# Two position biases: built on the chip and expanded through DRAM, or loaded as rows

## The chip, the cores and the metric

One core of one Trainium2 chip runs the whole program. The metric is the device time in microseconds (us) of one execution. The engines named below are PE (TensorE), DVE (VectorE), ACT (ScalarE), POOL (GpSimd) and SP (SyncE, which here only issues transfers).

## The reference

Two stacked models of width 1024 over 16 learned tokens and 256 input tokens. What matters here is the very first mixer, a gated linear attention (GLA), and the two attentions that add a bias by relative position to their logits:

```
# gated linear attention, chunks of 64 (the first layer)
proj = h @ w_in;  q, k, v, r = split(proj)
log_a = log_sigmoid((h @ w_a1) @ w_a2 + b_a) / 16
...
S = exp(tot) * S + (k * exp(tot - cum)).T @ v;  o = q @ S
# first attention (8 heads, top-64 keys): bias through 32 buckets
bias = rel_bias[rel_bucket(top_idx - qpos)]
# second attention (16 heads, band of chunks of 64)
idx = clip(qi + PAD - kj, MIN_REL, MAX_REL) - MIN_REL
bias = rel_bias_2[:, idx]
```

Both biases depend on the distance between query and key alone, so one line per head (8 lines and 16 lines) holds all of their values, and the bias of each query is a piece of that line, shifted by one element from query to query.

## The kernel before

**The weight stream.** All weights are cut into 386 units of 128 x 1024 float32 (512 KB). A unit goes through three stages: SP loads it into one of four slots of `w_raw` (line 370), ACT rounds it to `w_hi` (line 480), DVE computes the rest `w_lo` (line 1257), and PE does 24 matmuls with it (lines 856 to 858, eight tiles by three products). SP may load unit u+4 into a slot when `w_lo` of unit u is written. ACT and DVE prepare the unit that PE will use three units later (`ahead`). Every engine runs a list written out by hand, in that order: an engine that waits holds up everything behind it, and DVE reads PE's results (`scaled`, line 1273) in the same list in which it prepares weights.

**The first stages.** PE runs units `k` (4), `a1` (1), `v` (8), with four small matmuls `z` in the middle of `v` (line 912), and `q` (4). After the third unit of `q`, `to_tokens(0)` transposes the first chunk's keys and values (line 932). Then comes a loop over five chunks: state matmuls (line 949), `to_tokens` of the next chunk, one unit of `r` and the output matmuls (line 960). The state matmuls of a chunk wait until DVE has copied the transposes (line 1378) and read the last unit of `q` (`q_T`).

**The biases.** After `z`, PE expands `rel_bias` into `line1` (8 x 400, line 915), and DVE copies `line1` and builds `line2` (16 x 384) from `rel2`. POOL then stores each line 128 times into a DRAM scratch (lines 413 and 416), waits for both stores, and goes on with its additions of squares. Later POOL loads `bias1` and `bias2` (lines 427 and 456) from the scratch with an access pattern that starts one element earlier for each query (`skewed`). After `bias2` has landed POOL overwrites one part of it with a mask (line 460). `bm1` (line 438, first attention) and `lg2` (line 1802, second attention) use the biases.

The loads by SP go to the DMA queue q1 (hardware), those by POOL to q0 (software); both use the core's 16 DMA engines.

Of the kernel before, what the change touches and what calls it, by code (L numbers as in the profile page):

```python
# [14 lines left out]
F32 = mybir.dt.float32  # L15
# [6 lines left out]
P = 128  # L22
# [3 lines left out]
SEQ = 256  # L26
T = META + SEQ
# [7 lines left out]
ATT_HEADS = 8  # L35
# [3 lines left out]
HEADS2, HD2 = 16, 64  # L39
NREL2 = 192  # L40
# [1 line left out]

CHUNKS = [(0, META)] + [(META + CHUNK * c, META + CHUNK * (c + 1)) for c in range(SEQ // CHUNK)]
LINE1 = 400
LINE2 = 384
NEG_INADMISSIBLE = -1.0e38
NEG_TAKEN = -3.0e38
MASKED = -1.0e30
# [41 lines left out]

C_ID, C_GSEL, C_HSEL, C_PAIR, C_GBRD = 0, 128, 160, 288, 290
C_HBRD = C_GBRD + 512
C_BUCKET = C_HBRD + 1024
NCONST = C_BUCKET + LINE1


def shape_constants():
    c = np.zeros((P, NCONST), np.float32)
    c[:, C_ID:C_ID + P] = np.eye(P)
    for m in range(KD):  # L100
        c[:, C_GSEL + 4 * m + m // 2] = 1.0
        for half in range(2):
            c[64 * half:64 * half + 64, C_HSEL + 16 * m + 2 * m + half] = 1.0
            c[2 * m + half, C_HBRD + P * m + 64 * half:C_HBRD + P * m + 64 * half + 64] = 1.0
    for half in range(2):
        c[64 * half:64 * half + 64, C_PAIR + half] = 1.0
    for g in range(4):
        c[g, C_GBRD + P * g:C_GBRD + P * (g + 1)] = 1.0
    nb, max_exact, max_dist = 16, 8, 128
    for j in range(LINE1):  # L110
        rel = j - (T - 1)
        n = abs(rel)
        large = max_exact + int(np.float32(np.log(np.float32(max(n, 1)) / np.float32(max_exact)))
                                / np.float32(np.log(max_dist / max_exact)) * (nb - max_exact))
        b = (nb if rel > 0 else 0) + (n if n < max_exact else min(large, nb - 1))
        c[b, C_BUCKET + j] = 1.0
    return c


def build(nc, hT, weights, cols, w_a2, rel_bias, rel2_reversed, constants, outT):  # L120
    ctx = ExitStack()
    with ctx:
        def sb(name, shape, dt=F32):
            return ctx.enter_context(nc.sbuf_tensor(name, shape, dt))
# [8 lines left out]
        h = sb("h", [P, KD, T])  # L133
# [10 lines left out]
        con = sb("con", [P, NCONST])  # L144
# [3 lines left out]
        spl = sb("spl", [P, KD])  # L148
        coef = sb("coef", [P, KD])
        a2 = sb("a2", [RANK, GLA_HEADS * GLA_DK])  # L150
        relb = sb("relb", [32, ATT_HEADS])
        rel2 = sb("rel2", [HEADS2, NREL2])
        line1 = sb("line1", [ATT_HEADS, LINE1])
        line2 = sb("line2", [HEADS2, LINE2])
        ident = con[:, C_ID:C_ID + P]

        def region():
# [59 lines left out]
        bias1 = get("bias1", [P, ATT_HEADS, T])  # L217
# [52 lines left out]
        bias2 = get("bias2", [P, HEADS2, SEQ])  # L270
# [16 lines left out]
        pt = bank("pt")  # L287
# [6 lines left out]

        line1_dram = nc.dram_tensor("line1_dram", (ATT_HEADS, P, LINE1), F32).ap()
        line2_dram = nc.dram_tensor("line2_dram", (HEADS2, P, LINE2), F32).ap()

        def skewed(dram, heads, width, keys):  # L300
            return bass.AP(dram.tensor, P - 1, [[width - 1, P], [P * width, heads], [1, keys]])

        raw_loaded = [sem(f"raw_loaded{s}") for s in range(RING)]
        hi_ready = sem("hi_ready")
        lo_ready = sem("lo_ready")
# [3 lines left out]
        in_loaded = sem("in_loaded")  # L309
# [11 lines left out]
        def s_(name):  # L321
            if name not in sems:
                sems[name] = sem(name)
            return sems[name]
# [29 lines left out]
        @block.sync  # L354
        def _(sp):
            sp.dma_start(par[:, :], cols).then_inc(s_("par_loaded"), 16)
            sp.dma_start(w_raw[:, 0, :], weights[0, :, :]).then_inc(raw_loaded[0], 16)
            for quarter in range(4):
                n = slice(2 * quarter, 2 * quarter + 2)
                sp.dma_start(h[:, n, :], hT[:, n, :]).then_inc(h_loaded[quarter], 16)  # L360
            for u in range(1, RING):
                sp.dma_start(w_raw[:, u, :], weights[u, :, :]).then_inc(raw_loaded[u], 16)
            sp.dma_start(con[:, :], constants).then_inc(in_loaded, 16)
            sp.dma_start(a2[:, :], w_a2).then_inc(in_loaded, 16)
            sp.dma_start(relb[:, :], rel_bias).then_inc(in_loaded, 16)
            sp.dma_start(rel2[:, :], rel2_reversed).then_inc(in_loaded, 16)
            with sp.Fori(1, UNITS // RING) as i:
                for s in range(RING):
                    sp.wait_ge(lo_ready, i * RING + (s + 1 - RING))
                    sp.dma_start(w_raw[:, s, :], weights[bass.ds(i * RING + s, 1), :, :]  # L370
                                 .rearrange("a p n -> p (a n)")).then_inc(raw_loaded[s], 16)
            for u in range(UNITS // RING * RING, UNITS):
                sp.wait_ge(lo_ready, u + 1 - RING)
                sp.dma_start(w_raw[:, u % RING, :], weights[u, :, :]).then_inc(raw_loaded[u % RING], 16)
            for quarter in range(4):
                n = slice(2 * quarter, 2 * quarter + 2)
                sp.wait_ge(acc_free, tile_read("mlp1_out", 2 * quarter + 1))
                sp.dma_start(outT[:, n, :], h[:, n, META:T]).then_inc(s_("out_stored"), 16)
            sp.wait_ge(s_("out_stored"), 64)
# [3 lines left out]
        def _(pool):  # L383
            allt, xt = slice(0, T), slice(META, T)

            def add_squares(norm, tok):
# [22 lines left out]
                                           ALU.add).then_inc(s_("sqg_added"), 1)  # L409

            add_squares("mix0", allt)
            pool.wait_ge(s_("line1_ready"), 1)
            pool.dma_start(line1_dram, line1[:, :].rearrange("h (a w) -> h a w", a=1).to_broadcast([ATT_HEADS, P, LINE1]))\
                .then_inc(s_("line_stored"), 16)
            pool.wait_ge(s_("line2_ready"), 3)
            pool.dma_start(line2_dram, line2[:, :].rearrange("h (a w) -> h a w", a=1).to_broadcast([HEADS2, P, LINE2]))\
                .then_inc(s_("line_stored"), 16)
            pool.wait_ge(s_("line_stored"), 32)
            for c, (lo, hi) in enumerate(CHUNKS):
                pool.wait_ge(s_("osq_ready"), c + 1)  # L420
                pairs = o_sq[:, :, lo:hi].rearrange("p (g two) t -> p g two t", two=2)
# [2 lines left out]
            add_squares("ffn0", allt)  # L424
            add_squares("mix1", allt)
            pool.wait_ge(units_used, FIRST["dsa_c"])
            pool.dma_start(bias1[:, :, :], skewed(line1_dram, ATT_HEADS, LINE1, T))\
                .then_inc(s_("bias1_loaded"), 16)
            for t in range(2 * ATT_HEADS):
                hd, qt = t // 2, t % 2  # L430
# [22 lines left out]
            for norm in ("mlp0", "att2"):  # L453
                add_squares(norm, xt)
            pool.wait_ge(units_used, FIRST["kv2"])
            pool.dma_start(bias2[:, :, :], skewed(line2_dram, HEADS2, LINE2, SEQ))\
                .then_inc(s_("bias2_loaded"), 16)
            pool.wait_ge(s_("bias2_loaded"), 16)

            pool.memset(bias2[0:64, :, 192:256], MASKED).then_inc(s_("bias2_ready"), 1)  # L460

            for k in range(HEADS2):
                n = SEQ if k % 2 else P
# [382 lines left out]
        def _(pe):  # L846
# [58 lines left out]
            unit(FIRST["a1"], FIRST["a1"] % RING, pa[0][:, 0:T], x_hi, x_lo, allt, True, True)  # L905
            four("v", 0, MT["v"], 0, 0, x_hi, x_lo, allt)
            pe.wait_ge(s_("a1_ready"), 1)
            pe.wait_ge(in_loaded, 64)
            for n in range(4):
                if n >= 2:  # L910
                    pe.wait_ge(s_("z_ready"), n - 1)
                nc.tensor.matmul(pa[n % 2][:, 0:T], a2[:, n * P:(n + 1) * P], a1_T[:, :], start=True, stop=True)\
                    .then_inc(s_("z_psum"), 1)

            nc.tensor.matmul(pt[0:ATT_HEADS, 0:LINE1], relb[:, :], con[0:32, C_BUCKET:C_BUCKET + LINE1],
                             start=True, stop=True).then_inc(s_("line1_psum"), 1)
            four("v", 4, MT["v"] + 4, 0, 0, x_hi, x_lo, allt)

            def project_r(k):
# [23 lines left out]
            for c, (lo, hi) in enumerate(CHUNKS):  # L943
# [4 lines left out]
                for g in range(GLA_HEADS):  # L948
# [3 lines left out]
                                     start=True, stop=True).then_inc(s_("S_psum"), 1)  # L952
# [299 lines left out]
        def _(dve):  # L1252
# [81 lines left out]
            for k in range(8):  # L1334
# [1 line left out]
                scaled(v_T[:, k, :], acc[k % 4][:, 0:T], allt)  # L1336
                ahead("v", k)
                if k == 3:
                    dve.wait_ge(in_loaded, 64)
                    for n in range(4):  # L1340
                        dve.wait_ge(s_("z_psum"), n + 1)
                        V.tensor_scalar(z[:, n, :], pa[n % 2][:, 0:T], col("b_a", n), None, ALU.add)\
                            .then_inc(s_("z_ready"), 1)
                    dve.wait_ge(s_("line1_psum"), 1)
                    V.tensor_copy(line1[:, :], pt[0:ATT_HEADS, 0:LINE1]).then_inc(s_("line1_ready"), 1)

                    V.tensor_copy(line2[:, P - 1:P - 1 + NREL2], rel2[:, :]).then_inc(s_("line2_ready"), 1)
                    V.tensor_copy(line2[:, 0:P - 1], rel2[:, 0:1].to_broadcast([HEADS2, P - 1]))\
                        .then_inc(s_("line2_ready"), 1)
                    V.memset(line2[:, P - 1 + NREL2:LINE2], 0.0).then_inc(s_("line2_ready"), 1)  # L1350
                elif k == 5:
                    dve.wait_ge(s_("ln_ready"), 1)

# [428 lines left out]
                copy_values(g)  # L1782
            dve.wait_ge(s_("q2std_ready"), 1)
            own_wait(dve, V.reciprocal(q2rs[:, :], q2std[:, :]))
            dve.wait_ge(s_("bias2_ready"), 1)

            def trail_heads(m):
                dve.wait_ge(s_("o2_hi_ready"), m + 1)
# [132 lines left out]
def prepare(inputs):  # L1921
    inp = {k: np.asarray(v) for k, v in inputs.items()}
    tokens = np.concatenate([inp["meta"], inp["x"][0]], axis=0)
    arrays = {
        "hT": np.ascontiguousarray(tokens.T.reshape(KD, P, T).transpose(1, 0, 2)),
        "weights": weight_stream(inp),
        "cols": parameter_columns(inp),
        "w_a2": np.ascontiguousarray(inp["gla_w_a2"][0]),
        "rel_bias": np.ascontiguousarray(inp["rel_bias"]),
        "rel2_reversed": np.ascontiguousarray(inp["b_rel_bias_2"][0][:, ::-1]),  # L1930
        "constants": shape_constants(),
    }
    return arrays
# [19 lines left out]
```

## Time and profile before

| | |
|---|---|
| median of 3 runs | 1330.34 us (1328.74 to 1331.99) |
| span of the profiled execution | 1327.7 us |
| median less that span | 2.6 us |
| PE busy | 1267.2 us, 95% |
| DVE busy | 842.3 us, 63% |
| ACT busy | 679.1 us, 51% |
| POOL busy | 106.9 us, 8% |
| moved by DMA | 213.11 MB, mean 161 GB/s |

The profile is one execution; its device time isn't listed apart from its span, so the three runs stand for it, and the 2.6 us are what lies around the span and between executions. PE's share alone says that the kernel is bound by PE; where PE stands still or runs at the lower clock is seen only by stretches.

### The profile page before, as it was taken

How to read it: one execution, taken by the hardware profiler on the slowest of the kernel's cores; microseconds unless marked ns; L12 is line 12 of the kernel's file. 1: busy time of each engine (PE TensorE's matmuls, PEld its weight loads, DVE VectorE, ACT ScalarE, POOL GpSimd, SP SyncE). 2: the span in 40 equal slices, each digit the busy share in tenths (PEclk: the TensorE clock that was granted, in tenths of full speed). 3: DMA queues.
4: the chain of work that ended last, by engine and by line, in shares of the span. 5: the costliest groups of instructions: out<-in, count | busy, mean ns of one | idle time of the engine just before them, and what ended most of it. 6: DMA issues, size and time to landing. Idle time of an engine off the chain costs nothing.

```text
span 1327.7 us, 27055 instructions
## 1 busy us (share of the span) xinstructions
PE 1267.2 (95%) x9838; PEld 1218.5 (92%) x9838; DVE 842.3 (63%) x1310; ACT 679.1 (51%) x1096; POOL 106.9 (8%) x119
## 2 busy tenths in 40 slices
PE   8949999999999899999999869999999998999999
PEld 8939899999999679999999769999999876999998
DVE  6626776666557847666667897665556565766543
ACT  5413565554444535666555756554445346665432
POOL 2000010000100111000021121000000012100000
PEclk9969899999999859999999989999999988999999
DMA  7784355555665304556664446556567421555653
GB/s 252 128 160 114 103 169 174 171 172 184 190 208 159 96 0 144 176 187 189 191 201 149 142 128 189 188 180 188 179 184 241 142 78 33 176 188 185 196 179 105
DMA packets 59485, 213.11 MB, mean 161 GB/s; under 512 B 6776, under 2 KB 7944, under 8 KB 59296
## 3 DMA queue, kind: packets, MB, share of 16 engines
q1 hardware_dynamic: 57216, 204.26, 48.8%
q0 software_dynamic: 2208, 8.00, 4.0%
q8 instruction: 42, 0.69, 0.2%
q14 instruction: 19, 0.16, 0.0%
HBM read 206.40 MB, written 5.83 MB: 160 GB/s over the span
## 4 chain that ended last, share of the span: by engine, by line
PE 84%; DVE 8%; issue 2%; DMA 2%; ACT 2%; POOL 1%; SPq 0%; DVEq 0%; POOLq 0%; ACTq 0%
PE acc L856 25%; PE acc L858 25%; PE acc L857 25%; DMA w_raw<-weights 2%; DVE w_lo L1257 2%; PE acc L1084 2%; PE pa L1058 1%; PE acc L949 1%; PE pa L960 1%; POOL sqsum L403 1%; DVE t_s L1680 1%; DVE x_lo L1279 0%; DVE score L1545 0%; PE stat L1074 0%; PE pa L1182 0%
## 5 line engine op out<-in xcount | busy, mean ns | idle before, releaser
L1257 DVE TENSOR_TENSOR w_lo<-w_raw,w_hi 128x1024 fp32r<-128x1024 f32 x383 | 468.6, 1225 | 104.5 <-ACT w_hi L480 104.2
L856 PE MATMUL acc<-x_hi,w_hi 128*128 128x256 f32 (+1 forms) x1792 | 515.1, 287 | 15.3 <-DVE w_lo L1257 12.1
L480 ACT CAST w_hi<-w_raw 128x1024 fp32r<-128x1024 f32 x383 | 398.8, 1045 | 232.8 <-PE acc L858 188.0
L858 PE MATMUL acc<-x_hi,w_lo 128*128 128x256 f32 (+1 forms) x1792 | 511.0, 285 | 0.0
L857 PE MATMUL acc<-x_lo,w_hi 128*128 128x256 f32 (+1 forms) x1792 | 510.7, 285 | 0.0
L856 PEld LDWEIGHTS acc<-x_hi,w_hi 128*128 128x128 f32 x1792 | 341.1, 190 | 22.4 <-issue 15.5
L858 PEld LDWEIGHTS acc<-x_hi,w_lo 128*128 128x128 f32 x1792 | 341.3, 190 | 0.0
L857 PEld LDWEIGHTS acc<-x_lo,w_hi 128*128 128x128 f32 x1792 | 339.8, 190 | 0.3
L857 PE MATMUL acc<-m_lo,w_hi 128*128 128x256 f32 x512 | 144.9, 283 | 0.0
L858 PE MATMUL acc<-m_hi,w_lo 128*128 128x256 f32 x512 | 144.6, 282 | 0.0
L856 PE MATMUL acc<-m_hi,w_hi 128*128 128x256 f32 x512 | 143.5, 280 | 0.0
L857 PE MATMUL acc<-mid_lo,w_hi 128*128 128x272 f32 (+1 forms) x352 | 100.2, 285 | 0.0
L856 PE MATMUL acc<-mid_hi,w_hi 128*128 128x272 f32 (+1 forms) x352 | 100.1, 284 | 0.0
L858 PE MATMUL acc<-mid_hi,w_lo 128*128 128x272 f32 (+1 forms) x352 | 100.0, 284 | 0.0
L856 PEld LDWEIGHTS acc<-m_hi,w_hi 128*128 128x128 f32 x512 | 97.4, 190 | 0.0
L858 PEld LDWEIGHTS acc<-m_hi,w_lo 128*128 128x128 f32 x512 | 96.1, 188 | 0.0
L857 PEld LDWEIGHTS acc<-m_lo,w_hi 128*128 128x128 f32 x512 | 95.7, 187 | 0.0
L1297 DVE TENSOR_TENSOR h<-h,acc 128x256 f32 (+1 forms) x56 | 23.8, 426 | 97.3 <-PE acc L858 97.0
L497 ACT ACTIVATE sq<-h (+1 forms) x64 | 26.4, 422 | 95.8 <-DVE h L1297 95.8
L858 PEld LDWEIGHTS acc<-mid_hi,w_lo 128*128 128x128 f32 x352 | 66.4, 189 | 0.0
L857 PEld LDWEIGHTS acc<-mid_lo,w_hi 128*128 128x128 f32 x352 | 66.2, 188 | 0.0
L856 PEld LDWEIGHTS acc<-mid_hi,w_hi 128*128 128x128 f32 x352 | 66.0, 188 | 0.0
(303 smaller groups left out, 1641.3 us busy)
## 6 DMA issues: line engine op xcount, KB each, us to landing
w_raw<-weights SPq DMA_DIRECT2D x383, 512.0 KB, 3.5
line_dram<-line POOLq DMA_DIRECT2D x1, 3072.0 KB, 69.4
bias<-line_dram POOLq DMA_DIRECT2D x1, 2048.0 KB, 13.7
line_dram<-line POOLq DMA_DIRECT2D x1, 1600.0 KB, 36.5
con<-constants SPq DMA_DIRECT2D x1, 1113.0 KB, 9.6
h<-hT SPq DMA_DIRECT2D x4, 272.0 KB, 4.6
bias<-line_dram POOLq DMA_DIRECT2D x1, 1088.0 KB, 9.1
outT<-h SPq DMA_DIRECT2D x4, 256.0 KB, 4.8
```

Of the source, the lines that this page charges most:

```text
L403: pool.tensor_tensor(flat(sqsum[:, tok]), sq[:, bass.ds(n, 1), tok], flat(sqsum[:, tok]), ALU.add)\
L480: nc.scalar.copy(w_hi[:, slot, :], w_raw[:, slot, :]).then_inc(hi_ready, 1)
L497: nc.scalar.activation(sq[:, nn, tok], h[:, nn, tok], ACT.Square).then_inc(sq_ready, 1)
L856: nc.tensor.matmul(out, wh, xh[:, k, tok], start=first and n == 0, stop=False)
L857: nc.tensor.matmul(out, wh, xl[:, k, tok], start=False, stop=False)
L858: ins = nc.tensor.matmul(out, wl, xh[:, k, tok], start=False, stop=last and n == ntiles - 1)
L949: nc.tensor.matmul(acc[2 + g // 2][:, (g % 2) * GLA_DV:(g % 2 + 1) * GLA_DV], k_tok[0:n, c % 2, g * P:(g + 1) * P], v_tok[0:n, c % 2, g * ...
L960: ins = nc.tensor.matmul(pa[1][:, m * n:(m + 1) * n], S[:, c % 2, m // 2, (m % 2) * P:(m % 2 + 1) * P], q_T[:, m // 2, lo:hi], start=True, ...
L1058: nc.tensor.matmul(pa[qt][:, 0:n], q1[:, hd, qt * P:(qt + 1) * P], kh[:, hd, 0:n], start=True, stop=True).then_inc(s_("qk1"), 1)
L1084: ins = nc.tensor.matmul(acc[hd % 4][:, qt * P:(qt + 1) * P], vh[0:m, b, hd * P:(hd + 1) * P], pt1[0:m, qt, b0:b0 + P], start=(b == 0), st ...
L1257: V.tensor_tensor(w_lo[:, slot, :], w_raw[:, slot, :], w_hi[:, slot, :].bitcast(F32), ALU.subtract)\
L1297: V.tensor_tensor(h[:, nn, tok], h[:, nn, tok], acc[j][:, 0:n_tok].rearrange("p (a t) -> p a t", a=1), ALU.add)\
```

## The change

The host lays both biases out per query and head (`bias1_rows` 128 x 8 x 272, `bias2_rows` 128 x 16 x 256, the mask included) and passes them as inputs. POOL loads them at the same two places of its list as before. The PE matmul for `line1`, DVE's four instructions for the lines, the two stores, POOL's wait for them, the two small loads `relb` and `rel2` and the mask's memset are gone. The constants lose the 400 columns that `line1` needed (1113 KB before, 913 KB after, by their shapes of 128 x 2226 and 128 x 1826). DVE waits for `bias2_loaded` where it waited for `bias2_ready`.

```diff
+def skewed_biases(rel_bias, rel2):
+    at = (P - 1) - np.arange(P)[:, None] + np.arange(T)[None, :]
+    bias1 = rel_bias[bucket_line()[at]].transpose(0, 2, 1)
+    at = np.clip(np.arange(SEQ)[None, :] - np.arange(P)[:, None], 0, NREL2 - 1)
+    bias2 = rel2[:, ::-1][:, at].transpose(1, 0, 2).copy()
+    bias2[0:64, :, 192:256] = MASKED
+    return bias1, bias2
...
-            sp.dma_start(relb[:, :], rel_bias).then_inc(in_loaded, 16)
-            sp.dma_start(rel2[:, :], rel2_reversed).then_inc(in_loaded, 16)
...
-            pool.wait_ge(s_("line1_ready"), 1)
-            pool.dma_start(line1_dram, line1[:, :].rearrange("h (a w) -> h a w", a=1).to_broadcast([ATT_HEADS, P, LINE1]))\
-                .then_inc(s_("line_stored"), 16)
-            pool.wait_ge(s_("line2_ready"), 3)
-            pool.dma_start(line2_dram, line2[:, :].rearrange("h (a w) -> h a w", a=1).to_broadcast([HEADS2, P, LINE2]))\
-                .then_inc(s_("line_stored"), 16)
-            pool.wait_ge(s_("line_stored"), 32)
...
             pool.wait_ge(units_used, FIRST["dsa_c"])
-            pool.dma_start(bias1[:, :, :], skewed(line1_dram, ATT_HEADS, LINE1, T))\
+            pool.dma_start(bias1[:, :, :], bias1_rows)\
                 .then_inc(s_("bias1_loaded"), 16)
...
             pool.wait_ge(units_used, FIRST["kv2"])
-            pool.dma_start(bias2[:, :, :], skewed(line2_dram, HEADS2, LINE2, SEQ))\
+            pool.dma_start(bias2[:, :, :], bias2_rows)\
                 .then_inc(s_("bias2_loaded"), 16)
-            pool.wait_ge(s_("bias2_loaded"), 16)
-
-            pool.memset(bias2[0:64, :, 192:256], MASKED).then_inc(s_("bias2_ready"), 1)
...
-            nc.tensor.matmul(pt[0:ATT_HEADS, 0:LINE1], relb[:, :], con[0:32, C_BUCKET:C_BUCKET + LINE1],
-                             start=True, stop=True).then_inc(s_("line1_psum"), 1)
...
-                    dve.wait_ge(s_("line1_psum"), 1)
-                    V.tensor_copy(line1[:, :], pt[0:ATT_HEADS, 0:LINE1]).then_inc(s_("line1_ready"), 1)
-
-                    V.tensor_copy(line2[:, P - 1:P - 1 + NREL2], rel2[:, :]).then_inc(s_("line2_ready"), 1)
...
-            dve.wait_ge(s_("bias2_ready"), 1)
+            dve.wait_ge(s_("bias2_loaded"), 16)
```

POOL's list at the place of the stores, before (`z` here is the tile `o_sq2`, the sums of squares of the chunk loop; `line` and `line_dram` are the lines and the scratch):

```order
L400 COMPARE_AND_BRANCH
L413 DMA line_dram<-line 1024x1x400
L416 DMA line_dram<-line 2048x1x384
L422 TENSOR_TENSOR z<-o_sq 128x4x16
L422 TENSOR_TENSOR z<-o_sq 128x4x64 x4
```

and after:

```order
L400 COMPARE_AND_BRANCH
L415 TENSOR_TENSOR z<-o_sq 128x4x16
L415 TENSOR_TENSOR z<-o_sq 128x4x64 x4
L395 TENSOR_TENSOR sqsum<-sq 128x272
L400 UNCONDITIONAL_BRANCH
```

Both stores are gone, and nothing takes their place. DVE's list behind the four `z` instructions, before:

```order
L1345 COPY line<-pt 8x400
L1347 COPY line<-rel 16x192
L1348 COPY line<-rel 16x127
L1350 MEMSET line 16x65
L1273 TENSOR_TENSOR v_T<-acc,rstd 128x272
L1257 TENSOR_TENSOR w_lo<-w_raw,w_hi 128x1024
```

and after:

```order
L1261 TENSOR_TENSOR v_T<-acc,rstd 128x272
L1245 TENSOR_TENSOR w_lo<-w_raw,w_hi 128x1024
L1261 TENSOR_TENSOR v_T<-acc,rstd 128x272
L1245 TENSOR_TENSOR w_lo<-w_raw,w_hi 128x1024
L1335 SCALAR_TENSOR_TENSOR z<-z,zabs 128x1088
```

The four instructions for the lines are gone, and the rest keeps its order.

## Rows read from the trace of the kernel before

**Rows 1.** The chain that ended last, in order of time: start us, us, what.
```profile
44.05 0.77 PE pt L915 x2
...
57.49 31.66 DMA w_raw<-weights
...
106.05 1.92 PE acc L949 x8
...
114.16 1.92 PE acc L949 x8
```

**Rows 2.** DMA issues of the page: KB each, us from issue to landing.
```profile
w_raw<-weights SPq DMA_DIRECT2D x383, 512.0 KB, 3.5
line_dram<-line POOLq DMA_DIRECT2D x1, 3072.0 KB, 69.4
bias<-line_dram POOLq DMA_DIRECT2D x1, 2048.0 KB, 13.7
line_dram<-line POOLq DMA_DIRECT2D x1, 1600.0 KB, 36.5
...
bias<-line_dram POOLq DMA_DIRECT2D x1, 1088.0 KB, 9.1
```

**Rows 3.** DMA queues, 46 to 67 us: packets, MB, share of 16 engines.
```profile
q0 software_dynamic: 743, 1.84, 87.2%
q1 hardware_dynamic: 3, 0.01, 0.1%
```

**Rows 4.** Loads of weights issued between 52 and 64 us.
```profile
DMA to landing us min/median/max: 23.1/29.9/34.4
```

**Rows 5.** Waits, 40 to 125 us: us in total, times, longest.
```profile
POOL z L422 <- DMA line_dram<-line: 68.4, 1, 68.4
...
PE acc L949 <- DVE q_T L1273: 10.5, 1, 10.5
...
PE acc L856 <- DVE w_lo L1257: 9.1, 1, 9.1
```

**Rows 6.** Timeline, 66 to 100 us: start us, us, engine, what, [idle before].
```profile
68.39 0.60 PE L932 MATMUL stat<-con,v_T 128*16 128x128 f32 x4
...
78.09 0.57 PE L856 MATMUL acc<-x_hi,w_hi 128*128 128x272 f32 x1 [9.11 <-DVE w_lo L1257]
...
82.91 0.29 PE L858 MATMUL acc<-x_hi,w_lo 128*128 128x272 f32 x1
...
90.24 1.23 DVE L1257 TENSOR_TENSOR w_lo<-w_raw,w_hi 128x1024 fp32r<-128x1024 f32 x1 [5.03 <-ACT w_hi L480]
...
93.66 3.77 PE L949 MATMUL acc<-v_tok,k_tok 16*128 16x256 f32 x8 [10.46 <-DVE q_T L1273]
```

**Rows 7.** Windows: busy of PE, PEld, DVE, ACT, POOL; granted clock, DMA share, GB/s.
```profile
30.00:40.00 10.00, 10.00 (x81) 10.00 (x80) 5.03 (x7) 3.16 (x3) 0.00 (x0) 1.00 0.71 227
...
78.00:83.30 5.30, 5.10 (x24) 4.91 (x24) 0.30 (x1) 0.74 (x1) 0.00 (x0) 0.60 0.99 217
...
93.60:106.00 12.40, 12.34 (x61) 10.67 (x61) 5.94 (x12) 3.48 (x4) 0.00 (x0) 0.63 0.63 120
106.00:114.20 8.20, 8.20 (x62) 7.63 (x62) 5.41 (x12) 2.15 (x6) 0.00 (x0) 1.00 0.61 117
```

**Rows 8.** Loads of weights issued between 990 and 1015 us, beside `bias2`'s load.
```profile
DMA to landing us min/median/max: 3.5/4.5/8.3
```

**Rows 9.** Waits, 990 to 1120 us.
```profile
ACT w_hi L480 <- DMA w_raw<-weights: 0.5, 1, 0.5
```

**Rows 10.** Instructions on `bias1` and `bias2`: duration ns min/median/max, first and last start.
```profile
L438 POOL TENSOR_TENSOR bm<-bias,mask x16: 487/756/1317, 439.5 to 484.3; 128x144 f32<-128x144 f32 x8, 128x272 f32<-128x272 f32 x8
L1802 DVE SCALAR_TENSOR_TENSOR lg<-pa,q2rs,bias x16: 340/342/351, 1080.9 to 1106.0; 128x128 f32<-128x128 f32 x16
...
L427 POOL DMA_DIRECT2D bias<-line_dram x1: 923/923/923, 381.4 to 381.4; - x1
L456 POOL DMA_DIRECT2D bias<-line_dram x1: 1202/1202/1202, 995.5 to 995.5; - x1
```

More of the change, by code:

```diff
@@ L44 @@
 LINE1 = 400
-LINE2 = 384
 NEG_INADMISSIBLE = -1.0e38
@@ L92 @@
 C_HBRD = C_GBRD + 512
-C_BUCKET = C_HBRD + 1024
-NCONST = C_BUCKET + LINE1
+NCONST = C_HBRD + 1024
 def shape_constants():
@@ L108, in shape_constants, with bucket_line @@
         c[g, C_GBRD + P * g:C_GBRD + P * (g + 1)] = 1.0
+    return c
+def bucket_line():
+    buckets = np.zeros(LINE1, np.int64)
     nb, max_exact, max_dist = 16, 8, 128
@@ L115, in shape_constants, with build @@
         b = (nb if rel > 0 else 0) + (n if n < max_exact else min(large, nb - 1))
-        c[b, C_BUCKET + j] = 1.0
-    return c
-def build(nc, hT, weights, cols, w_a2, rel_bias, rel2_reversed, constants, outT):
+        buckets[j] = b
+    return buckets
+def skewed_biases(rel_bias, rel2):
[5 more added lines that the diff above has]
+    return bias1, bias2
+def build(nc, hT, weights, cols, w_a2, bias1_rows, bias2_rows, constants, outT):
     ctx = ExitStack()
@@ L150, in build @@
         a2 = sb("a2", [RANK, GLA_HEADS * GLA_DK])
[L151 to L154, printed above, removed]
         ident = con[:, C_ID:C_ID + P]
@@ L293, in build @@
         trans1 = [pt, stat]
[L297 to L301, printed above, removed]
         raw_loaded = [sem(f"raw_loaded{s}") for s in range(RING)]
@@ L907, in _ @@
             pe.wait_ge(s_("a1_ready"), 1)
-            pe.wait_ge(in_loaded, 64)
+            pe.wait_ge(in_loaded, 32)
             for n in range(4):
@@ L1338, in _ @@
                 if k == 3:
-                    dve.wait_ge(in_loaded, 64)
+                    dve.wait_ge(in_loaded, 32)
                     for n in range(4):
@@ L1343, in _ @@
                             .then_inc(s_("z_ready"), 1)
-                    dve.wait_ge(s_("line1_psum"), 1)
-                    V.tensor_copy(line1[:, :], pt[0:ATT_HEADS, 0:LINE1]).then_inc(s_("line1_ready"), 1)
-                    V.tensor_copy(line2[:, P - 1:P - 1 + NREL2], rel2[:, :]).then_inc(s_("line2_ready"), 1)
-                    V.tensor_copy(line2[:, 0:P - 1], rel2[:, 0:1].to_broadcast([HEADS2, P - 1]))\
-                        .then_inc(s_("line2_ready"), 1)
-                    V.memset(line2[:, P - 1 + NREL2:LINE2], 0.0).then_inc(s_("line2_ready"), 1)
                 elif k == 5:
@@ L1923, in prepare @@
     tokens = np.concatenate([inp["meta"], inp["x"][0]], axis=0)
+    bias1, bias2 = skewed_biases(inp["rel_bias"], inp["b_rel_bias_2"][0])
     arrays = {
@@ L1928, in prepare @@
         "w_a2": np.ascontiguousarray(inp["gla_w_a2"][0]),
-        "rel_bias": np.ascontiguousarray(inp["rel_bias"]),
-        "rel2_reversed": np.ascontiguousarray(inp["b_rel_bias_2"][0][:, ::-1]),
+        "bias1_rows": np.ascontiguousarray(bias1),
+        "bias2_rows": np.ascontiguousarray(bias2),
         "constants": shape_constants(),
```

## The prediction

> **What bounds the kernel now.** I read the page first, then the chain of waits that ended last, then the stretch of that chain that isn't matmuls. PE is busy for 95% of the span, and nearly all of the chain is PE's stream of weight units, so instructions off PE are worth nothing by themselves. The exception stands out in the chain in order of time: one piece of 31.66 us at 57.49 us that is a DMA, a load of weights [rows 1]. An ordinary load of weights lands in 3.5 us [rows 2]. The reader is to see that this piece begins about 10 us after POOL has issued the two stores of the bias lines, and ends while the longer one is still under way (69.4 us to landing) [rows 2].
>
> The DMA view of 46 to 67 us tells why. POOL's queue q0 moved 743 packets and took 87.2% of the 16 engines; SP's queue q1, with the weights, moved 3 packets [rows 3]. The four loads issued between 52 and 64 us landed after 23.1 to 34.4 us [rows 4]. So the stores did not slow the weights down, they kept them out.
>
> The list of waits says who paid. The longest wait, POOL's 68.4 us for the stores, is a decoy: what POOL does next is needed by PE only at the end of the chunk loop. What costs are PE's waits of 9.1 us (for `w_lo`) and 10.5 us (for `q_T`, which stands on DVE behind `w_lo` instructions that wait for late weights) [rows 5]. The timeline gives the places: PE ends `to_tokens(0)` at 68.39 + 0.60 = 68.99, starts the last unit of `q` at 78.09, ends it at 82.91 + 0.29 = 83.20, and starts the state matmuls of chunk 0 at 93.66 [rows 6]. Those of chunk 1 start at 106.05 [rows 1]. Beside the waits there is the clock: 0.60 of full speed in 78.0 to 83.3 us and 0.63 in 93.6 to 106.0, right behind PE's two long pauses, and 1.00 from 106 us on [rows 7]. 0.60 is a mix of the levels 1.2 and 2.4 GHz.
>
> **The change, part by part.** Between 68.99 and 106.05 lie 37.06 us. With the weights on time the same work costs:
>
> - The wait of 9.10 us before the last unit of `q`: none. With loads that land in 3.5 us its weights are there by about 56 us, and `w_lo` follows on DVE's list right after the first `q_T`, before PE is through with the third unit. Saved 9.1.
> - The unit itself: 83.20 - 78.09 = 5.11 us, partly at the lower clock. At full clock 81 matmuls took 10.00 us [rows 7], so 24 take 3.0. Saved 2.1.
> - The pause of 10.46 us before the state matmuls. DVE has three copies of transposes and the last `q_T` to do there, on its list behind one `w_lo`. From that `w_lo` (90.24) to PE's start (93.66) it took 3.4 us [rows 6]: the pause becomes at least 0 and at most 3.4. The `w_lo` and most of the copies can run while PE is in the unit (3.0 us), so only `q_T` is left behind it, and I take 0.5. Saved 10.0.
> - Chunk 0: 106.05 - 93.66 = 12.39 us, against 114.16 - 106.05 = 8.11 us for chunk 1 [rows 1], with the same number of state matmuls, transposes, unit and output matmuls at the full clock. Saved 4.3.
>
> That is 25.5 us. To it comes the `line1` matmul, 0.77 us on the chain itself [rows 1]: the `v` unit behind it starts that much earlier, and everything up to `to_tokens(0)` with it, because DVE and ACT are ahead of PE there. Saved 0.8. Together 26.3.
>
> The rest is costed at nothing. DVE's four instructions for the lines lie under PE's next unit. The 200 KB less of constants, and the two small loads, lie under a start that waits for the sums of squares. The mask's memset and the moved wait for `bias2` lie far ahead of their readers: `bias2` has landed by 995.5 + 13.7 = 1009.2 and is read at 1080.9; `bias1` has landed by 381.4 + 9.1 = 390.5 and is read at 439.5 [rows 2, 10]. The loads could take 49 us and 71 us longer before a reader waits; the cover gone, each further us would cost one. What they can do is hold up weights. The load of `bias2` did so a little: weights beside it took up to 8.3 us [rows 8], and ACT waited 0.5 us for one of them [rows 9], PE not at all. So ACT has 8.3 - 0.5 = 7.8 us of cover for a landing. The bytes are the same after the change, the rows longer (8.7 and 16 KB in one piece, where pieces of about 1 KB were read). No row shows such a load on POOL's queue; between a gain of nothing (PE doesn't wait there now) and the rival's price below, I take 0, since both loads before stand next to it in everything but the length of rows.
>
> **The sum.** Span 1327.7 - 26.3 = 1301.4. The median of the runs is 2.6 us above that span, so 1304.0 for the changed kernel.
>
> One rule is to be weighed here. The row shows 3 packets of weights against 743 of the stores [rows 3]. The Trainium skill, page "DMA: Bandwidth & Descriptors", section "Queues, rings and completion order", says that each DMA engine goes round the queues for which it has work, packet by packet. By that rule the weights would have had every second turn even then, the lateness would have another cause, and the sum would shrink towards the 0.8 us of the matmul. This trace disagrees with it for stores, by the 3 packets.
>
> **The rivals.**
>
> 1. *The new loads keep the weights out as the stores did* (weights of `dsa_c` and `kv2`). For: [rows 3] shows that POOL's queue can do it. Against: its loads of the same bytes did not, with at most 8.3 us for a unit. If weights stood still for the whole 9.1 and 13.7 us, they would be late by 9.1 + 3.5 - 7.8 = 4.8 and 13.7 + 3.5 - 7.8 = 9.4 us at ACT, 14.2 together; two units already prepared for PE take up to 6.0 us of each, which leaves 0 and 3.4. Time 1307 to 1318, say 1313. Chance 5%.
> 2. *The clock doesn't come back.* The last unit of `q` and chunk 0 follow on short matmuls of 16 rows and a short pause, and could run at the lower clock still. Then 2.1 and 4.3 us are not saved: 1310.4. For: both places were low. Against: chunk 1 and later run the same mix at 1.00 [rows 7], and the long pauses ahead of both are gone. Chance 8%.
> 3. *The stores aren't the cause.* The loads would be late because SP's queue stalls by itself, and the change doesn't do what it says. Only 0.8 us would go: 1329.5. Against: loads land in 3.5 us elsewhere. Chance 1%.
> 4. *Slower.* The direct loads could move at the pace of the stores, with the weights shut out. That pace was 1.84 MB in 21 us, 88 GB/s [rows 3]: 1.11 MB and 2.10 MB would take 12.7 and 23.9 us, and ACT would be late by 8.4 and 19.6, 28.0 together and 1.7 more than is saved: 1332.0. Under 85 GB/s the kernel would be slower by over 0.2%. Against: the loads landed at 122 and 153 GB/s, with weights moving beside them [rows 2, 8]. Chance 1%.
>
> **How the numbers follow.** The forecast itself has 85%. Its range: the pause before chunk 0 (-0.5 to +2.9 us), the bias loads (0 to 3.4), where PE's short spells of the lower clock fall once all is shifted (some 2 us either way, an estimate from the 2.1 us of one unit), and the scatter of the runs (1328.74 to 1331.99, so 1.6 us to either side). That gives 1300.5 to 1309.5; rival 2 lies just outside, and 1300 to 1310 leaves out no more than 2 in 10. About 0.2% (2.7 us) is what a measurement of this kernel tells from no change. Faster is the forecast with rivals 1 and 2, 98%; the same is rival 3, 1%; slower is rival 4, 1%.
>
> **What would show it.** After the change the loads of weights between 45 and 110 us should land in 3.5 to 6 us; no DMA piece of over 5 us should stand in the chain there; PE's two waits of 9.1 and 10.5 us should be gone, with at most one of under 3.4 us before the first state matmuls; those of chunk 1 should start at about 79.8 us; the clock should be near 1.00 from 68 to 80 us; and all that follows should stand about 26 us earlier. ACT's waits for weights beside the two bias loads should stay under 1 us. I would be wrong if weights are still late without any store (rival 3), if PE waits near 357 or 970 us (the bias loads, shifted), or if DVE's list (the scan of `cum`, the copies) rather than the weights turns out to hold the first state matmuls.

## The result, and the profile after

The changed kernel takes 1291.3 us (median of 4 runs, 1289.29 to 1292.38), the kernel before 1331.16 (4 runs, 1328.74 to 1332.22): a ratio of 0.970, 95% interval 0.969 to 0.972. The forecast was 1304, with a range of 1300 to 1310. The sign was right, the size was not: 40 us were gained where 26.3 were forecast.

The page of the kernel after, with its shares, its matmuls on `m`, and its DMA issues (KB each, us from issue to landing); the last three answer to [rows 2]:

```profile
span 1289.9 us, 27041 instructions
...
PE 1247.2 (97%) x9836; PEld 1200.1 (93%) x9836; DVE 842.0 (65%) x1306; ACT 678.5 (53%) x1096; POOL 102.9 (8%) x116
...
L848 PE MATMUL acc<-m_hi,w_lo 128*128 128x256 f32 x512 | 141.3, 276 | 0.0
...
w_raw<-weights SPq DMA_DIRECT2D x383, 512.0 KB, 3.5
bias<-bias_rows POOLq DMA_DIRECT2D x1, 2048.0 KB, 8.8
...
bias<-bias_rows POOLq DMA_DIRECT2D x1, 1088.0 KB, 5.7
```

Loads of weights issued between 44 and 104 us, which answer to [rows 4], and the waits of the same stretch (us in total, times, longest), which answer to [rows 5]:

```profile
DMA to landing us min/median/max: 3.5/3.8/5.0
```

```profile
POOL z L415 <- ACT o_sq L560: 75.0, 3, 59.5
...
PE acc L937 <- DVE q_T L1261: 1.4, 1, 1.4
```

No weights are late, no engine waits for a DMA, and of PE's two long pauses 1.4 us are left. POOL waits about as long as before, now for something else: it was the decoy it seemed to be. The timeline of the same places as [rows 6], and the chain in order of time with chunk 1 (start us, us, what):

```profile
66.44 0.60 PE L920 MATMUL stat<-con,v_T 128*16 128x128 f32 x4
...
69.78 0.29 PE L848 MATMUL acc<-x_hi,w_lo 128*128 128x272 f32 x1
...
71.51 1.99 PE L937 MATMUL acc<-v_tok,k_tok 16*128 16x256 f32 x8 [1.44 <-DVE q_T L1261]
```

```profile
81.27 1.92 PE acc L937 x8
```

Chunk 1 begins at 81.27 us, where it began at 106.05 [rows 1]: 24.8 us earlier. Here the forecast was nearly right (79.8). But the end of the span is 1327.7 - 1289.9 = 37.8 us earlier, so 13.0 us came later, in a part of the kernel that the change was not supposed to touch. Windows show where. First the kernel before: two stretches that hold nothing but matmuls on the `m` tensors (the moving operand of the two MLPs' output stages), and the `xq` stage between them (here the moving operand of the second attention's output stage). The columns are those of [rows 7]; the count behind PE's busy time is what to read.

```profile
905.00:990.00 85.00, 85.00 (x711) 85.00 (x710) 44.39 (x44) 35.48 (x44) 5.58 (x6) 1.00 0.61 187
...
1236.00:1321.00 85.00, 85.00 (x711) 85.00 (x710) 37.25 (x36) 28.74 (x28) 0.00 (x0) 1.00 0.53 169
...
1116.00:1140.00 24.00, 24.00 (x188) 24.00 (x187) 16.21 (x21) 11.98 (x21) 5.45 (x6) 0.92 0.41 132
```

The same three places in the kernel after, and the two stretches from 68 to 88 us for chunk 0 and chunk 1:

```profile
68.00:80.00 12.00, 10.56 (x67) 9.42 (x66) 8.54 (x16) 2.33 (x2) 0.00 (x0) 0.86 0.51 172
80.00:88.00 8.00, 8.00 (x62) 7.47 (x61) 5.37 (x13) 1.81 (x4) 0.32 (x1) 1.00 0.20 66
...
882.00:962.00 80.00, 80.00 (x709) 80.00 (x708) 43.99 (x44) 35.56 (x43) 5.60 (x6) 1.00 0.61 195
...
1203.00:1283.00 80.00, 80.00 (x708) 80.00 (x707) 37.46 (x36) 28.90 (x28) 0.00 (x0) 1.00 0.56 180
...
1086.50:1107.00 20.50, 20.50 (x183) 20.50 (x183) 15.84 (x21) 11.62 (x21) 5.06 (x6) 1.00 0.48 151
```

PE is busy without a gap in all of these and its clock is full in both `m` stretches, yet a matmul is issued every 85.00 / 711 = 119.5 ns before and every 80.00 / 709 = 112.8 ns after. (A count takes in the two or three matmuls that the window's edges cut. Such a pace reads 0.3 to 0.4% low over 80 us and over 1% low over 20 us, so only windows of like length are compared.) There are 3 x 512 matmuls on `m`: 1536 x 6.7 ns = 10.3 us. In the `xq` stage 192 matmuls go from 24.00 / 188 = 127.7 ns to 20.50 / 183 = 112.0 ns: 3.0 us, of which the clock (0.92 to 1.00) makes 0.08 x 24.00 = 1.9 and the pace the rest. Together 13.3, which is the gain that was missing. The clock's part isn't tied to the places: the run moved by 64 bytes (below) has the slow pace and yet a clock of 1.00 in this stage. All other stages with weights keep their pace within 1%. The code and the shapes of `m` and `xq` are the same in both kernels; the one thing that the change does to them is to move them. It removes `relb` (32 bytes a partition), `rel2` (768), `line1` (1600), `line2` (1536) and 400 columns of `con` (1600 bytes): 5536 bytes. The trace doesn't record where a tensor lies; worked out from the kernel's tensors, in their order and sizes, everything allocated behind them lies 5536 bytes lower.

### The profile page after: what moved, and what is told of

It is laid out like the page before. It is cut to its first block, busy times and chain, and to the rows that moved or that the text cites. A ratio compares the mean times of both kernels' runs of the same rounds, so it can differ in the third digit from the quotient of the medians.

```text
span 1289.9 us, 27041 instructions
## 1 busy us (share of the span) xinstructions
PE 1247.2 (97%) x9836; PEld 1200.1 (93%) x9836; DVE 842.0 (65%) x1306; ACT 678.5 (53%) x1096; POOL 102.9 (8%) x116
## 4 chain that ended last, share of the span: by engine, by line
PE 85%; DVE 9%; issue 3%; ACT 2%; POOL 1%; DVEq 0%; POOLq 0%; ACTq 0%
PE acc L846 26%; PE acc L848 25%; PE acc L847 25%; DVE w_lo L1245 2%; PE acc L1072 2%; PE pa L1046 1%; PE acc L937 1%; PE pa L948 1%; POOL sqsum L403 1%; DVE t_s L1661 1%; DVE x_lo L1267 0%; DVE score L1526 0%; PE stat L1062 0%; PE pa L1170 0%; ACT w_hi L470 0%
## 5 line engine op out<-in xcount | busy, mean ns | idle before, releaser
L848 PE MATMUL acc<-m_hi,w_lo 128*128 128x256 f32 x512 | 141.3, 276 | 0.0
L847 PE MATMUL acc<-m_lo,w_hi 128*128 128x256 f32 x512 | 141.3, 276 | 0.0
```

What stands on the lines that cost most here:

```text
L847: nc.tensor.matmul(out, wh, xl[:, k, tok], start=False, stop=False)
L848: ins = nc.tensor.matmul(out, wl, xh[:, k, tok], start=False, stop=last and n == ntiles - 1)
```

## The experiments

Two theories of the 40 us. *Stores only*: all of it comes from the stores that went, and the `m` stretches are faster by something that hangs on them. *Two parts*: the stores are worth 24 or so, and the places of the tensors 13 or so. And for the stores: which property of them kept the weights out (queue, size, length of rows, repetition, few source partitions)? The kernels ran in three groups, each beside the kernel before on the same chip, which had medians of 1329.3, 1332.15 and 1331.71 us (7 runs each); a difference between groups holds to about 2 us. A "pace" below is a window's us by its count of matmuls, as above.

### Stores and places apart

**The code of before, with the places of after.** The lines' tensors and the bucket columns become tensors at the end of the first stage's region, so that all others lie where the kernel after has them.

```diff
-        con = sb("con", [P, NCONST])
+        con = sb("con", [P, NKEPT])
-        relb = sb("relb", [32, ATT_HEADS])      # and rel2, line1, line2
...
+        buckets = get("buckets", [32, LINE1])   # behind ga_lo
+        relb = get("relb", [32, ATT_HEADS])     # and rel2, line1, line2
...
+            sp.dma_start(buckets[:, :], constants[0:32, C_BUCKET:NCONST]).then_inc(in_loaded, 16)
```

> The kernel before with its stores, matmul and skewed loads, but the small tensors (relb, rel2, line1, line2 and the 400 bucket columns) moved out of the way, so that every other SBUF tensor sits at the address that it has in the changed kernel. Theory S+P (stores cost 25 us, placement of the matmuls' operands the other 12 to 13): 1318 us, with m_hi and xq_hi matmuls at 113 ns from start to start and weights still late around 57 to 90 us. Rival (the whole gain of 40 us is from the stores and what follows from them, such as the clock): 1331 us.

Measured: 1314.13 us (4 runs, 1312.47 to 1317.6), ratio 0.988 (0.986 to 0.990). Its window of the `m` matmuls, and its waits from 40 to 125 us:

```profile
905.00:985.00 80.00, 80.00 (x708) 80.00 (x708) 44.64 (x45) 36.24 (x45) 5.59 (x6) 1.00 0.62 192
```

```profile
POOL z L425 <- DMA line_dram<-line: 66.0, 1, 66.0
ACT w_hi L483 <- DMA w_raw<-weights: 37.1, 6, 11.3
...
PE acc L952 <- DVE q_T L1276: 9.4, 1, 9.4
...
PE acc L859 <- DVE w_lo L1260: 9.2, 1, 9.2
```

The stores and both of PE's pauses are there as before, and yet 15.2 us are gained and the `m` matmuls run at 113.0 ns.

**The code of after, with the places of before.**

```diff
         a2 = sb("a2", [RANK, GLA_HEADS * GLA_DK])
+        spare = sb("spare", [P, 1384])
```

> The changed kernel with 5536 unused bytes per partition ahead of the stages' tensors, so that these sit where they sat before the change. Theory S+P: 1303 to 1304 us, m_hi and xq_hi matmuls at 120 ns from start to start as before the change, and the weights on time. Rival (all from the stores): 1291 us, matmuls at 113 ns.

Measured: 1305.33 us (4 runs, 1304.63 to 1305.66), ratio 0.982 (0.980 to 0.984). The window of its `m` matmuls:

```profile
880.00:965.00 85.00, 85.00 (x711) 85.00 (x710) 44.36 (x44) 36.43 (x44) 5.58 (x6) 1.00 0.59 185
```

A tensor that nobody reads or writes costs 1305.3 - 1291.3 = 14.0 us (the kernel after was measured beside a kernel before of 1331.2 us, not of 1329.3; by the ratios, 0.982 and 0.970, it is some 15). The four corners agree: places are worth 15.2 us with the stores and 14.0 without; the stores are worth 1329.3 - 1305.3 = 24.0 us at the old places and 1314.1 - 1291.3 = 22.8 at the new. *Stores only* falls.

### What about a place counts

The same edit with other sizes, one run each, and once with a gap ahead of the weights' tensors, which moves `w_raw`, `w_hi` and `w_lo` too, and all that lies between them and `a2`:

```diff
+        spare = sb("spare", [P, 8])             # shift_32; 16, 48 and 64 for 64, 192 and 256 bytes
```
```diff
+        gap0 = sb("gap0", [P, 16])              # weights_shift_64, ahead of w_raw
...
+        spare = sb("spare", [P, 48])            # and 192 bytes behind a2
```

> The changed kernel with 32 unused bytes ahead of the stages' tensors. If a start at an odd multiple of 32 bytes is what slowed the m and xq matmuls before, they run at about 120 ns again and the time is about 1303 us. If the place within 1024 bytes, or the part of SBUF, decides, they stay near 113 ns and the time near 1291 us.

> The changed kernel with 64 unused bytes ahead of the stages' tensors, so that they start at multiples of 64 again but elsewhere within 128 to 1024 bytes. Theory A (an operand that starts at an odd multiple of 32 bytes is slow, multiples of 64 are fast): m matmuls at 113 ns from start to start, time 1291 us. Theory B (the place within 1024 bytes counts, and 832 was a lucky one): m at 117 to 120 ns, 1301 to 1304 us.

> The changed kernel with 256 unused bytes ahead of the stages' tensors. Theory C (what counts is the place of an operand's row within 256 bytes: 64 is fast, 96, 128 and 224 were 118 to 120 ns): m and xq matmuls at 113 ns as without the shift, about 1291 us. Rival (a longer period, or the part of SBUF): 118 to 120 ns and 1303 us.

> The changed kernel with all tensors from w_raw on moved by 64 bytes, and the stages' tensors by 256, so that m_hi and xq_hi stay at 64 within 256 bytes while the weights w_hi and w_lo move from 128 to 192. If the place of the moving operand alone counts: m at 113 ns. If its distance to the weights counts: m as at 0 beside weights at 128, which no run has shown, so anything but 113 ns says that it does.

> The changed kernel with 192 unused bytes ahead of the stages' tensors: m and xq at 0 within 256 bytes, the place that is missing. Under theory C a pace of its own between 113 and 120 ns, the same in both m stages; time 1291 to 1304 us.

Measured: 1303.43 (32 bytes), 1304.59 (64), 1292.84 (256), 1303.01 (weights moved by 64, `m` by 256) and 1304.66 us (192). The windows of the `m` matmuls, of 32, 64, 256 bytes, of the moved weights, and of 192 bytes:

```profile
880.00:964.00 84.00, 84.00 (x712) 84.00 (x711) 44.43 (x45) 36.05 (x44) 5.59 (x6) 1.00 0.59 191
```
```profile
882.00:967.00 85.00, 85.00 (x711) 85.00 (x710) 44.24 (x45) 35.98 (x44) 5.59 (x6) 1.00 0.56 186
```
```profile
880.00:960.00 80.00, 80.00 (x708) 80.00 (x707) 44.02 (x45) 35.92 (x44) 5.60 (x6) 1.00 0.62 197
```
```profile
882.00:967.00 85.00, 85.00 (x718) 85.00 (x717) 44.40 (x44) 36.03 (x45) 5.57 (x6) 1.00 0.60 189
```
```profile
880.00:965.00 85.00, 85.00 (x719) 85.00 (x718) 45.13 (x45) 36.46 (x44) 5.57 (x6) 1.00 0.59 189
```

A shift by 256 bytes changes nothing; 32 and 64 bytes cost 12 and 13 us. So the pace repeats after 256 bytes, as far as this one shift shows. The run that moved the weights by 64 bytes left `m` where it was but for 256 bytes, and still lost the fast pace. It has the pace of the last run, in which the weights stayed and `m` moved by 192 (118.4 and 118.2 ns). What these two share is the distance between the moving operand and the weights, not the address of either. (The gap moved other tensors with the weights, but of those PE reads only the weights in this stage.)

| place of `m` less place of the weights, modulo 256 bytes | kernel | ns per matmul of `m` |
|---|---|---|
| 192 | after; moved by 256; before's code at after's places | 112.8; 113.0; 113.0 |
| 224 | moved by 32 | 118.0 |
| 128 | moved by 192; weights moved by 64 | 118.2; 118.4 |
| 96 | before; after's code at before's places | 119.5; 119.5 |
| 0 | moved by 64 | 119.5 |

The stages `at` (output of the first attention) and `lr` (output of the recurrent layer) moved too, and so test the same distances on other tensors. Four windows of 16 us at full clock: first distance 192, `at` of the run moved by 32 and `lr` of after's code at before's places; then distance 96, `at` of the run moved by 192 and `lr` of the run moved by 64:

```profile
482.00:498.00 16.00, 16.00 (x144) 16.00 (x142) 13.55 (x18) 9.88 (x19) 4.76 (x6) 1.00 0.58 187
768.00:784.00 16.00, 16.00 (x143) 16.00 (x142) 14.84 (x20) 10.67 (x19) 4.74 (x5) 1.00 0.65 202
```
```profile
482.00:498.00 16.00, 16.00 (x136) 16.00 (x135) 13.52 (x17) 9.57 (x18) 4.75 (x6) 1.00 0.63 189
768.00:784.00 16.00, 16.00 (x135) 16.00 (x135) 14.32 (x19) 10.54 (x18) 4.75 (x5) 1.00 0.67 203
```

Counts of 144 and 143 against 136 and 135: these stages are fast and slow at the same distances as `m`.

**Rows of 1280 bytes.** The operands `x` and `mid` have rows of 1088 bytes (272 columns), so that their rows lie at all of four places in turn, and a window of the `x` matmuls shows 115 us / 974 = 118.1 ns in both kernels. With rows of 1280 bytes each row would have the same place.

```diff
+ROW = 320
-        x_hi = sb("x_hi", [P, KD, T], F32R)
+        x_hi = sb("x_hi", [P, KD, ROW], F32R)   # and x_lo, mid_hi, mid_lo
```

> The changed kernel with rows of 1280 bytes in place of 1088 for x_hi, x_lo, mid_hi and mid_lo (the last 192 bytes of each row unused), so that all rows of an operand start at the same place within 256 bytes, as those of m_hi do. Theory A2 (the x and mid matmuls run at 118 and 126 ns because the place of the row changes from tile to tile): x at 256 columns falls to 113 ns, at 272 columns to about 120, and the kernel gains 20 us (1271 us). Rival (only the 64 bytes count, and x is slow for another reason): 1291 us.

Measured: 1292.66 us (4 runs), ratio 0.971 (0.969 to 0.973): no gain over the kernel after. The `x` matmuls, whose rows now all start at distance 64, run at 115 / 979 = 117.5 ns, hardly faster than the 118.1 of rows at four places:

```profile
505.00:620.00 115.00, 115.00 (x979) 115.00 (x978) 77.18 (x122) 70.08 (x92) 0.00 (x0) 1.00 0.57 183
```

Its two `m` stretches are the surprise:

```profile
880.00:960.00 80.00, 80.00 (x709) 80.00 (x708) 43.48 (x44) 35.55 (x43) 5.61 (x6) 1.00 0.61 196
...
1200.00:1284.00 84.00, 84.00 (x716) 84.00 (x715) 37.58 (x36) 29.00 (x28) 0.00 (x0) 1.00 0.54 171
```

Both use the same tensors at the same place, distance 192. One ran at 112.8 ns, the other at 84.00 / 716 = 117.3. So this distance has two paces, and the address alone doesn't decide. It isn't the only case. Two more windows of 16 us at distance 192, `lr` of the kernel before and `xq` of before's code at after's places, have counts of 138, between the 144 and the 136 above:

```profile
790.00:806.00 16.00, 16.00 (x138) 16.00 (x138) 14.86 (x21) 10.39 (x18) 4.77 (x5) 1.00 0.69 223
```
```profile
1114.00:1130.00 16.00, 16.00 (x138) 16.00 (x138) 13.33 (x18) 9.80 (x18) 4.09 (x5) 1.00 0.51 158
```

`xq` of the kernel after, at the same places, ran fast (143 matmuls in 1088 to 1104 us).

**All operands at that distance.** Rows of 1280 bytes and five gaps of 32 to 192 bytes put the 256-column operands `x`, `mid`, `m`, `xq`, `at` and `lr` 192 bytes past the weights (the few matmuls of the recurrent layer's gates, on `xc`, stay at 32).

```diff
+        gap0 = sb("gap0", [P, 32])              # ahead of x_hi; gap1 behind a2
+        gap2 = get("gap2", [P, 48])             # ahead of mid_hi; gap3 at_hi; gap4 lr_hi
```

> The changed kernel with rows of 1280 bytes for x_hi, x_lo, mid_hi and mid_lo and small gaps, so that the 256-column matmuls of x, mid, m, xq, at and lr all start at 64 within 256 bytes (the 272-column ones of x and mid at 0). Theory C: x and mid at 256 columns go from 118.3 to 113.4 ns, which is worth 17 us, at and lr 2 us; the 272-column ones are unknown (120 to 127 ns, so -8 to +1 us): 1264 to 1280 us. If 64 has a second, slower pace of 117.8 ns, as the second m stage of the kernel with rows of 1280 bytes showed, up to all of it is lost: 1291 us.

Measured: 1285.19 us median (1275.42, 1282.56, 1287.82, 1295.7), ratio 0.968 (0.963 to 0.973). The fastest of these runs was profiled. Its windows of an `x` stage and of the `m` matmuls:

```profile
505.00:620.00 115.00, 115.00 (x1017) 115.00 (x1017) 81.05 (x128) 72.78 (x96) 0.00 (x0) 1.00 0.62 192
...
870.00:950.00 80.00, 80.00 (x708) 80.00 (x707) 43.40 (x44) 35.56 (x43) 5.63 (x6) 1.00 0.62 195
```

The `x` matmuls too can run at 115.00 / 1017 = 113.1 ns, and a whole execution of 1275.4 us is possible, 16 us under the median of the kernel after and 14 under its fastest run. But the four runs spread over 20 us, where those of the kernel after spread over 3, and the intervals of the two ratios overlap. It is a promise, not a better kernel shown.

### What about the stores kept the weights out

Three versions of the kernel after with a store added at the place where the lines' stores were: on POOL's queue, 4352 KB in all, with POOL waiting for it as before. What is stored is `h`, which nobody reads back.

```diff
+            pool.wait_ge(s_("z_ready"), 4)
+            for copy in range(4):               # wide_stores
+                pool.dma_start(wide_dram[copy].rearrange("k p t -> p k t"), h[:, :, :]).then_inc(s_("line_stored"), 16)
+            pool.dma_start(store_dram, h[0:16, 0:1, :].to_broadcast([16, 256, T]))     # narrow_stores
+            pool.dma_start(store_dram, h[0:128, 0:1, :].to_broadcast([128, 32, T]))    # repeat_stores
```

> The changed kernel with four stores of h (128 partitions, rows of 1088 bytes, 4352 KB in all) into DRAM issued by POOL where the two stores of the lines (8 and 16 partitions, 4672 KB) stood; the output is the same. If any store of that size on POOL's queue shuts the weights out, about 25 us are lost again (1316 us). If it was the lines' few source partitions that made the stores slow and kept the engines occupied, the stores land in some 20 us and at most 5 us are lost (1291 to 1296 us).

> The changed kernel with one store of 4352 KB from 16 partitions of h, each row of 1088 bytes repeated 256 times, where the stores of the lines stood; the output is the same. If few source partitions make the stores slow and keep the engines from the weights: the store takes 50 us or more to land, weights come 20 us late, and some 23 us are lost (1314 us). Rival (it was the row length or the second DMA behind the first): 1292 us.

> The same store of 4352 KB, each row of 1088 bytes repeated 32 times, from all 128 partitions of h. If it is the number of source partitions that counts, this one lands in about 17 us as the wide stores did, and the time is 1292 us. If a repeated source row is what is slow, it is as bad as the narrow one (1314 us).

Measured: 1291.79 (wide), 1315.14 (narrow) and 1289.19 us (repeat), one run each. The DMA queues from 46 to 67 us, as in [rows 3], of wide, narrow and repeat:

```profile
q0 software_dynamic: 1088, 4.46, 63.8%
q1 hardware_dynamic: 672, 2.45, 28.6%
```
```profile
q0 software_dynamic: 423, 1.84, 84.2%
q1 hardware_dynamic: 115, 0.41, 4.7%
```
```profile
q0 software_dynamic: 1040, 4.46, 62.7%
q1 hardware_dynamic: 578, 2.09, 24.4%
```

And the issues of narrow from 46 to 67 us, then those of repeat:

```profile
store_dram<-h POOLq DMA_DIRECT2D x1, 4352.0 KB, 49.0
w_raw<-weights SPq DMA_DIRECT2D x4, 512.0 KB, 28.0
```
```profile
store_dram<-h POOLq DMA_DIRECT2D x1, 4352.0 KB, 20.5
w_raw<-weights SPq DMA_DIRECT2D x5, 512.0 KB, 9.6
```

Same queue, same bytes, same rows of 1088 bytes, the same kind of repeated source. Read from 16 partitions it takes 49.0 us, holds the weights up for 28.0 us, and gives back the whole gain of the stores (1315.1 - 1291.3 = 23.8 us). Read from 128 partitions it takes 20.5 us, the weights land after 9.6, and the kernel loses nothing. So what counts is the source: few partitions, each repeated often. `line1` was stored from 8 partitions and `line2` from 16. The number of repeats changed with the partitions (256 against 32) and wasn't tried apart; against it as the cause stands that the lines' stores, with 128 repeats of each row, moved the same 1.84 MB in the same 21 us [rows 3] as the narrow store with 256.

## Why the prediction was off

**Right: what bound the start, and that it would go.** By its own steps, chunk 1 was forecast 26.3 us earlier and came 24.8 earlier:

- The wait of 9.1 us before the last unit of `q` is gone, and the unit takes 70.07 - 67.04 = 3.03 us (forecast 3.0).
- The pause before the state matmuls is 1.44 us, where 0.5 was taken and 0 to 3.4 allowed.
- Chunk 0 takes 81.27 - 71.51 = 9.76 us, not 8.11. The clock in 68 to 80 us is 0.86, not 1.00: rival 2, in part. Costs 1.65.
- The `line1` matmul was given 0.8 us. `to_tokens(0)` ends 1.95 us earlier (67.04 against 68.99), although the stretch starts 0.3 us later. The rest, 1.45, is clock, which the prediction had not looked at. In the kernel before the granted clock was 0.50 from 45 to 48 us, the lower level of 1.2 GHz, right behind short matmuls of 16 and 32 rows (those for `z` and the one for `line1`); in the kernel after, with those for `z` alone, it stayed at 1.00, 2.4 GHz. First the window of before, then one of after:

```profile
46.00:47.00 1.00, 1.00 (x7) 1.00 (x6) 0.00 (x0) 0.99 (x2) 1.00 (x2) 0.50 0.00 0
```
```profile
46.00:48.00 2.00, 2.00 (x18) 2.00 (x17) 0.39 (x1) 1.97 (x4) 0.00 (x0) 1.00 0.00 0
```

But this difference doesn't belong to the `line1` matmul. After's code at before's places has no such matmul either, and its clock was 0.50 here; in 68 to 80 us, where the kernel after had 0.86, it was 1.00, and chunk 0 took 81.43 - 73.29 = 8.14 us, as forecast. Its two windows, and its chain at the start of chunks 0 and 1:

```profile
47.00:50.00 3.00, 3.00 (x15) 3.00 (x15) 0.00 (x0) 2.97 (x4) 0.00 (x0) 0.50 0.01 1
...
68.00:80.00 12.00, 11.46 (x89) 10.48 (x87) 9.39 (x16) 3.44 (x4) 0.00 (x0) 1.00 0.55 176
```
```profile
73.29 1.99 PE acc L938 x8
...
81.43 1.92 PE acc L938 x8
```

Where the short spells of the lower clock fall changes from run to run of almost the same code.

Sum: 26.3 - 0.3 + 1.45 - 0.94 - 1.65 = 24.9, against 24.8 read. That the total came so near the forecast is in part luck: four misses, two of them of the clock, cancel but for 1.4 us. The stores measured by themselves are worth 22.8 to 24.0 us. Of the rivals, 1, 3 and 4 fell: the new bias loads land in 5.7 and 8.8 us, sooner than the old ones (9.1 and 13.7, [rows 2]), and no instruction waits for them. Two sums of the prediction don't come out, without effect on the outcome: rival 4 leaves out the 6.0 us of cover by prepared units that rival 1 takes off each load (with it 2.4 + 13.6 = 16.0 us are lost, 1320 us, which isn't slower), and the terms of the range, added up, give 1299.9 to 1313.9, not 1300.5 to 1309.5.

**The step that failed** is "the rest is costed at nothing". The removed tensors and constants were costed as instructions and bytes to move, and that part was right. That their going moves every tensor behind them was not thought of; it was worth 14 to 15 us by the two kernels that differ in places alone, and no rival and no bound of the range held it. Without it the forecast would have stood: the code of after at before's places took 1305.3 us, against 1304.0 in the prediction. Why the pace follows the places stays open.

**The rule that was weighed.** The prediction set 3 packets of weights against 743 [rows 3] beside what the Trainium skill says on the page "DMA: Bandwidth & Descriptors", section "Queues, rings and completion order", that an engine goes round its queues packet by packet, and went by the row. The experiments show where the rule comes near and where it doesn't. With stores from 128 partitions the weights had 672 of 1760 and 578 of 1618 packets, over a third, where every second turn would be a half (weights were not waiting all the time); with a store from 16 partitions 115 of 538, while four loads stood waiting, and with the lines' stores 3 of 746. Turns counted in packets say nothing of how long one packet holds its engine. An estimate of that is the queue's share of 16 x 21 = 336 us by its packets: 0.67 us for a packet of the narrow store (84.2%, 423) and 0.20 for one of the wide stores (63.8%, 1088), though both are of 4.1 to 4.4 KB. This alone doesn't explain why the waiting weights had fewer packets than the store. In the narrow run all queues together moved 1.84 + 0.41 MB in 21 us, 107 GB/s, in the wide run 4.46 + 2.45 MB, 329 GB/s.

One more page bears on this. The Trainium skill, page "SBUF — State Buffer", section "Door 1: The DMA port swizzle", says that a transfer's rate follows from how many of the memory's ports its partitions reach, and gives 104 GB/s for partitions 0 to 15, which reach 4 of 16. The narrow store comes near it: 4352 KB in 49.0 us are 91 GB/s. That the engines sit occupied behind those few ports, with the weights queued behind them, fits both, but no run here looked into an engine.

## What to carry to other kernels

A store that repeats a few partitions many times is slow and, what is worse, keeps out the loads of another queue that the main engine lives on: spread its source over all 128 partitions, or give it to a stretch in which nothing is streamed (the second wasn't tried here). Removing or resizing a tensor is a change to every tensor behind it: before a gain or loss is put down to the edit, run the edit once with a dummy tensor of the removed size, and compare the ns per matmul of untouched stages. If PE is the bound, count the matmuls in a full window (us by count, windows of one length) of each stage; two stages of one shape at different paces hint at time to be had from placement.

## What the runs showed of the hardware

- The pace of back-to-back matmuls, each with its own load of weights, at full clock and without a gap, goes from 112.8 to 119.5 ns (6%) with the distance between the moving operand and the weights modulo 256 bytes. The Trainium skill, page "SBUF — State Buffer", section "Who interferes with whom", gives TensorE two independent read ports and says that it never waits on anyone. No run here looks at what other engines do to the pace. That the pace goes with the distance between TensorE's two operands speaks against reads that are free of each other; this is argued from the rows, and no run shows the mechanism.
- One distance (192) has two paces, 112.8 and 117.3 ns, in two stages of one execution on the same tensors; the slower one shows in the kernel before and in before's code at after's places too. What chooses stays open. Whether it makes the 20 us of spread of the kernel in which these operands have that distance isn't known, since only the fastest of its runs has a trace. Five distances of the eight multiples of 32 were tried for `m`, all but 192 and 96 with one or two kernels.
- 4352 KB from 16 partitions: 49.0 us, weights 28.0 us to landing. From 128: 20.5 and 9.6 us. Where between 16 and 128 the harm ends was not tried, nor the number of repeats by itself. Two rows of stores from few partitions, with 128 and with 256 repeats, show the same 1.84 MB in 21 us.
